# A two-step state space recurrence, and an fp32r scatter of the experts' results in two passes

## What is computed

```
def s5_mixer(u, lam_re, lam_im, b, c, d_skip, log_dt, w_glu, b_glu):   # 64 groups of 16 channels, 64 states each
    dt = exp(log_dt); a = exp((lam_re + 1j * lam_im) * dt)             # one complex factor per state
    b_bar = (a - 1) / lam * b
    x[t] = a * x[t - 1] + b_bar @ u[t]                                 # for 256 tokens t
    y[t] = real(c @ x[t]) + d_skip * u[t]
    g = gelu(y)
    val, gate = split(g @ w_glu + b_glu)
    return val * sigmoid(gate)

def moe_ffn(u, w_router, w13, w2):                                     # top 2 of 8 experts
    top_val, top_idx = top_k(u @ w_router, 2); top_w = softmax(top_val)
    out = 0
    for e in range(8):
        gate_e = sum(where(top_idx == e, top_w, 0))
        out += gate_e[:, None] * swiglu(u, w13[e], w2[e])
```

## Time and profile before

| | |
|---|---|
| median of 3 runs | 2593.39 us (2592.49 to 2596.54) |
| the profiled execution, its own time | 2592.58 us |
| its span in the trace | 2590.5 us, 31848 instructions |
| PE busy | 2421.6 us (93%) |
| DVE busy | 1809.1 us (70%) |
| ACT busy | 1261.3 us (49%) |
| POOL busy | 159.4 us (6%) |
| mean granted clock of PE | 0.961 of full speed |
| read from HBM | 583.60 MB, 226 GB/s over the span |

### The profile page before, as it was taken

How to read it: one execution, slowest core, us unless ns; L and a number is a source line. 1 busy time by engine, 2 the same in 40 slices (tenths; PEclk the granted TensorE clock), 3 DMA queues, 4 the chain that set the end, 5 groups by cost and what they waited for, 6 DMA issues and landing times.

```text
span 2590.5 us, 31848 instructions
## 1 busy us (share of the span) xinstructions
PE 2421.6 (93%) x12441; PEld 1937.3 (75%) x12441; DVE 1809.1 (70%) x1966; ACT 1261.3 (49%) x1290; POOL 159.4 (6%) x142
## 2 busy tenths in 40 slices
PE   7999999999999999989989965689999999999996
PEld 6878858788878678789658852367888887887885
DVE  5763348857852477685545459968888888898887
ACT  3432334334322434344334444537667677776674
POOL 0000000000000000000100006500000000000000
PEclk9999999999999999999999985789999999999998
DMA  9767158657756287543245530138999989998994
GB/s 315 257 230 181 50 180 287 248 205 274 258 162 150 66 280 272 195 170 115 98 155 188 178 121 33 65 122 281 336 338 345 347 319 348 350 343 323 344 345 176
DMA packets 303413, 586.14 MB, mean 226 GB/s; under 512 B 61439, under 2 KB 96965, under 8 KB 303181
## 3 DMA queue, kind: packets, MB, share of 16 engines
q1 hardware_dynamic: 285954, 521.09, 58.0%
q0 software_dynamic: 16928, 63.46, 7.4%
q10 hardware_dynamic: 428, 0.15, 0.0%
HBM read 583.60 MB, written 1.06 MB: 226 GB/s over the span
## 4 chain that ended last, share of the span: by engine, by line
PE 84%; DVE 10%; ACT 3%; issue 2%; DMA 1%; DVEq 0%; SPq 0%; ACTq 0%
PE psum L862 19%; PE psum L864 19%; PE psum L863 19%; PE psum L1326 3%; PE psum L895 3%; PE psum L1333 2%; PE psum L1388 2%; PE psum L2049 2%; PE psum L985 2%; DVE ring_r L1062 2%; PE psum L2673 2%; PE psum L2828 1%; PE psum L2851 1%; ACT ring_r L1056 1%; PE psum L1946 1%
## 5 line engine op out<-in xcount | busy, mean ns | idle before, releaser
L1062 DVE TENSOR_TENSOR ring_r<-ring,ring_r 128x2048 fp32r<-128x2048 f32 x286 | 652.6, 2289 | 291.4 <-ACT ring_r L1056 291.0
L1056 ACT CAST ring_r<-ring 128x2048 fp32r<-128x2048 f32 x286 | 545.2, 1910 | 507.3 <-PE psum L864 412.8
L864 PE MATMUL psum<-ring_r,arena_r 128*128 128x512 f32 (+1 forms) x1560 | 596.9, 383 | 0.0
L862 PE MATMUL psum<-ring_r,arena_r 128*128 128x512 f32 (+1 forms) x1016 | 400.3, 394 | 10.1 <-DVE arena_r L2846 5.2
L1062 DVE TENSOR_TENSOR ring_r<-ring,tail_r 128x2048 fp32r<-128x2048 f32 x143 | 327.2, 2288 | 95.9 <-ACT tail_r L1056 95.8
L863 PE MATMUL psum<-ring_r,arena_r 128*128 128x512 f32 (+1 forms) x1016 | 390.6, 384 | 0.0
L1056 ACT CAST tail_r<-ring 128x2048 fp32r<-128x2048 f32 x143 | 273.2, 1910 | 145.3 <-PE psum L864 139.3
L864 PEld LDWEIGHTS psum<-ring_r,arena_r 128*128 128x128 f32 x1560 | 294.4, 189 | 58.4
L864 PE MATMUL psum<-ring_r,z_r 128*128 128x512 f32 (+1 forms) x840 | 310.6, 370 | 0.0
L862 PEld LDWEIGHTS psum<-ring_r,arena_r 128*128 128x128 f32 x1016 | 192.3, 189 | 57.9 <-issue 18.5
L863 PEld LDWEIGHTS psum<-ring_r,arena_r 128*128 128x128 f32 x1016 | 192.3, 189 | 37.7 <-issue 1.9
(11 more groups left out here) (436 smaller groups left out, 3293.9 us busy)
## 6 DMA issues: line engine op xcount, KB each, us to landing
ring<-in_moe_w SPq DMA_DIRECT2D x264, 1024.0 KB, 6.9
arena<-in_ada_w POOLq DMA_DIRECT2D x48, 1024.0 KB, 9.2
ring<-in_ffn_wg SPq DMA_DIRECT2D x44, 1024.0 KB, 7.4
ring<-in_ffn_wu SPq DMA_DIRECT2D x44, 1024.0 KB, 7.3
ring<-in_ffn_wd SPq DMA_DIRECT2D x44, 1024.0 KB, 7.0
ring<-in_ffn_w SPq DMA_DIRECT2D x33, 1024.0 KB, 5.6
ring<-in_mlstm_w_in SPq DMA_DIRECT2D x8, 2048.0 KB, 8.6
ring<-in_mlstm_w_out SPq DMA_DIRECT2D x4, 2048.0 KB, 9.1
```

Source lines behind the costliest of these rows:

```text
L862: pe.matmul(dst, lhs_low, rhs, start=start, stop=False)
L864: return pe.matmul(dst, lhs, rhs_low, start=False, stop=stop)
L1056: act.copy(upper[i % UPPERS], place(PN[r.key, i])).then_inc(upper_ready, 1)
L1062: dve.tensor_tensor(low, raw, upper[i % UPPERS], ALU.subtract).then_inc(lower_ready, 1)
```

## The change

Two things are changed.

**The recurrence takes two tokens per step.** With PAIRS = 128, a state at an even token 2m follows from that at 2m - 2 with the squared factor, driven by `a b_bar u[2m - 1] + b_bar u[2m]`. So `inputs` now adds two products per state (with `BT` of two kinds, `b_bar` and `a b_bar`), and everything between it and `outputs` has 128 columns in place of 256: the phases, the rotations, DVE's four operations, the scans (now with `l_mag2`, the squared magnitude) and POOL's two products. The odd tokens are computed from the even ones: `y[2m + 1] = real(c a x[2m]) + real(c b_bar) u[2m + 1]`. POOL makes `c a` as `CT_next` (five operations per k, `c{k}`), PE makes the kernel `real(c b_bar)` (`same_step`, eight small matmuls, into `bank(7)`, which DVE clears once), ACT copies it (`copy_kernel`), and `outputs` has three parts: the even tokens (16 matmuls of 128 columns), one full matmul with the kernel, and the odd tokens (16 more, which wait for `c{k}`). `scanned` has eight places instead of four. `s5_scale_b_dve` is called with a piece 0 to 3, in `ffn_dve` of `ffn4` behind the half-panels 26 to 29, instead of all at once after `ffn4`, and makes twice as much (`b_wide` and `b_next`). The second half of the turned B (`bt4` to `bt7`) is made inside the recurrence. C's load waits for the end of `ffn4` instead of `bt3`. ACT's gelu of the first half stands earlier in its stream, the gated product uses other PSUM banks, and its second high half no longer waits for the last unit.

**The scatter is fp32r in two passes.** `scatter` is now a 0/1 matrix in fp32r; `y_part` is the high part of an expert's result and `y_low` the rest, which DVE subtracts (`lower_y_dve`, two operations per expert on a new semaphore `half_lowered`). `scatter_pe` issues four fp32r matmuls per half instead of two fp32 ones, and the gate is applied by DVE when it adds (`scattered_dve`). `route_dve` clears more.

The diff, cut to its core:

```diff
+            if r.n == 4 and "s5" in stages and UP_HALVES + 4 <= i < UP_HALVES + 8:
+                s5_scale_b_dve(dve, step, i - UP_HALVES - 4)
...
+        for out_, other, op in ((l_kr2, l_ki, ALU.subtract), (l_ki2, l_kr, ALU.add)):
+            dve.tensor_tensor(l_t1, l_lr, l_kr if out_ is l_kr2 else l_ki, ALU.mult)
+            link(dve.tensor_tensor(l_t2, l_sin, other, ALU.mult))
+            link(dve.tensor_tensor(out_, l_t1, l_t2, op))
...
+            if k >= 2 and n % 2 == 0:
                 pool.wait_ge(*s5P.after(f"y{k - 2}"))
-            pool.tensor_tensor(prods[k % 2][:, 0:2, j, :], scanned[:, n % 4, :, :, :], both(r[:, 0, :, :]), ALU.mult)
-            pool.tensor_tensor(prods[k % 2][:, 2:4, j, :], scanned[:, n % 4, :, :, :], both(r[:, 1, :, :]), ALU.mult)\
-                .then_inc(*s5G.inc(f"x{n}"))
+            pool.tensor_tensor(prods[:, k % 2, 0:2, j, :], scanned[:, n % 8], both(r[:, 0]), ALU.mult)
+            pool.tensor_tensor(prods[:, k % 2, 2:4, j, :], scanned[:, n % 8], both(r[:, 1]), ALU.mult).then_inc(*s5G.inc(f"x{n}"))
+            if n % 2 == 0:
+                continue
+            c, after = CT[:, k % 2], CT_next[:, k % 2]
+            pool.wait_ge(*s5A.after(f"ct{k}"))
+            if k >= 1:
+                pool.wait_ge(*s5G.after(f"c{k - 1}"))
+            pool.tensor_tensor(after, c, lam_of(l_lr, k, 3), ALU.mult)
+            pool.tensor_tensor(c_part, c[:, 0:2], lam_of(l_sin, k, 2), ALU.mult).then_inc(*step.one())
+            pool.wait_ge(*step.now())
+            pool.tensor_tensor(after[:, 0], after[:, 0], c_part[:, 1], ALU.add)
+            pool.tensor_tensor(after[:, 1], after[:, 1], c_part[:, 0], ALU.subtract)
+            pool.tensor_tensor(after[:, 2], after[:, 2], c_part[:, 1], ALU.subtract).then_inc(*s5G.inc(f"c{k}"))
...
-                act.activation(phase[:, j, :], const("steps"), ACT.Identity, scale=turns)
-                ins = act.activation(whole[:, j, :], const("steps"), ACT.Identity, scale=turns, bias=eps[:, 4:5])
+                act.activation(phase[:, j, :], steps, ACT.Identity, scale=turns)
+                ins = act.activation(whole[:, j, :], steps, ACT.Identity, scale=turns, bias=eps[:, 4:5])
...
+        def copy_kernel(k):
+
+            act.wait_ge(*s5P.after(f"kb{k}"))
+            act.copy(kernel_0[:, k % 2, :], bank(7)[:, SEQ:SEQ + P]).then_inc(*s5A.inc(f"kc{k}"))
...
             place_c(k)
+            if k >= 1:
+                copy_kernel(k - 1)
             if k + 1 < KD:
                 rotations(k + 1)
+            else:
+                gelu(act, 0)
+            if k == 0:
+                copy_b(6)
+                copy_b(7)
+        copy_kernel(KD - 1)
...
-            dve.scalar_tensor_tensor(xT[:, k, :], xT[:, k, :], col_a("s5_d", k), bank(6)[:, 0:SEQ], ALU.mult, ALU.add)\
+            steps_of = xT[:, k, :].rearrange("p (m i) -> p m i", i=2)
+            dve.scalar_tensor_tensor(steps_of, steps_of, col_a("s5_d", k),
+                                     bank(6 - k % 2)[:, 0:SEQ].rearrange("p (i m) -> p m i", i=2),
+                                     ALU.mult, ALU.add)\
...
-            dve.tensor_tensor(by_cos, bu, both(r[:, 0, :, :]), ALU.mult)
-            dve.tensor_tensor(bu, bu, both(r[:, 1, :, :]), ALU.mult).then_inc(*s5V.inc(f"w{n}"))
+            dve.tensor_tensor(cosines, bu, both(r[:, 0]), ALU.mult)
+            dve.tensor_tensor(bu, bu, both(r[:, 1]), ALU.mult).then_inc(*s5V.inc(f"w{n}"))
...
-                mag = l_mag[:, state:state + 1].to_broadcast([P, SEQ])
+                mag = l_mag2[:, state:state + 1].to_broadcast([P, PAIRS])
                 for i in range(2):
-                    ins = dve.tensor_tensor_scan(scanned[:, n % 4, i, jj, :], mag, bu[:, 1 - i, jj, :], 0.0, ALU.mult, ALU.add)
+                    ins = dve.tensor_tensor_scan(scanned[:, n % 8, i, jj, :], mag, bu[:, 1 - i, jj, :], 0.0, ALU.mult, ALU.add)
             ins.then_inc(*s5V.inc(f"scan{n}"))
-            if n % 2 and k >= 1:
-                skip_u(k - 1)
+            if n % 2 and k >= 2:
+                skip_u(k - 2)
...
         low_x(0)
+        skip_u(KD - 2)
         glu_lower_dve(dve, 0)
         skip_u(KD - 1)
...
-            pe.wait_ge(*s5A.after(f"ct{k}"))
             pe.wait_ge(*s5G.after(f"x{2 * k + 1}"))
-            if k >= 1:
-                pe.wait_ge(*s5V.after(f"y{k - 1}"))
+            if k < 2:
+                pe.wait_ge(*s5A.after("bt7"))
+            else:
+                pe.wait_ge(*s5V.after(f"y{k - 2}"))
+            even, odd = (bank(6 - k % 2)[:, i * PAIRS:(i + 1) * PAIRS] for i in range(2))
             for i, v in enumerate((0, 1, 1, 2)):
                 for j in range(QUAD):
-                    own_rows = slice(32 * j, 32 * j + 32)
-                    mm = pe.matmul(bank(6)[own_rows, 0:SEQ], CT[:, k % 2, v, j, :], prods[k % 2][:, i, j, :],
-                                   start=i == 0, stop=i == 3)
+                    pe.matmul(even[channels(j), :], CT[:, k % 2, v, j, :], prods[:, k % 2, i, j, :], start=i == 0, stop=i == 3)
+            pe.wait_ge(*s5A.after(f"kc{k}"))
+            pe.matmul(odd, kernel_0[:, k % 2, :], x_at[:, k, 1, :], start=True, stop=True)
+            pe.wait_ge(*s5G.after(f"c{k}"))
+            for i, v in enumerate((0, 1, 1, 2)):
+                for j in range(QUAD):
+                    mm = pe.matmul(odd[channels(j), :], CT_next[:, k % 2, v, j, :], prods[:, k % 2, i, j, :],
+                                   start=False, stop=True, skip_group_check=True)
             mm.then_inc(*s5P.inc(f"y{k}"))
...
+            pe.wait_ge(*s5A.after(f"ct{k}"))
+            if k >= 1:
+                pe.wait_ge(*s5A.after(f"kc{k - 1}"))
+            for part in range(2):
+                for j in range(QUAD):
+                    mm = pe.matmul(bank(7)[channels(j), SEQ + 32 * j:SEQ + 32 * j + 32],
+                                   b_wide[:, part, QUAD * k + j, :, :].rearrange("p g h -> p (g h)"), CT[:, k % 2, part, j, :],
...
+            for i in range(2):
+                for j in range(2):
+                    rows_ = channels(2 * u + j)
+                    pe.matmul(driven(n)[:, i, j, :], BT[rows_, 0, i, k, :], x_at[rows_, k, 0, :], start=True, stop=True)
+                for j in range(2):
+                    rows_ = channels(2 * u + j)
+                    mm = pe.matmul(driven(n)[:, i, j, 1:PAIRS], BT[rows_, 1, i, k, :], x_at[rows_, k, 1, 0:PAIRS - 1],
+                                   start=False, stop=True, skip_group_check=True)
...
+        for n in range(S5_UNITS + 1):
+            k, odd = divmod(n, 2)
             if n < S5_UNITS:
                 inputs(n)
-                if n % 2:
-                    turn_c(n // 2)
-            if n % 2 == 0 and n >= 4 and n // 2 - 2 < KD - 1:
-                outputs(n // 2 - 2)
+            if n in (0, 2):
+                for i in (4 + n, 5 + n):
+                    if n == 2:
+                        pe.wait_ge(*s5A.after(f"bt{i - 2}"))
+                    turn_b(pe, i)
+            if (odd or n == S5_UNITS) and k >= 1:
+                same_step(k - 1)
+            if odd:
+                turn_c(k)
+            elif k >= 2:
+                outputs(k - 2)
...
-        dve.memset(scatter, 0.0)
-        dve.memset(y_part, 0.0).then_inc(half_copied, 2)
-        dve.memset(y_sum[:, :, :], 0.0)
+        dve.memset(late_gate[:, :, 0:1], 0.0)
+        link(dve.memset(y_sum[:, :, :], 0.0))
+        dve.tensor_copy(scatter, y_sum[:, 0, 0:NT * P])
+        dve.tensor_copy(y_low, y_sum[:, 1, :])
+        dve.tensor_copy(y_part, y_sum[:, 1, :]).then_inc(half_lowered, 2)
...
-        pe.wait_ge(half_copied, 2 * e + (half + 1))
-        for t in range(NT):
-            mm = pe.matmul(bank((6, 4)[half] + t), scatter[:, t * P:(t + 1) * P], y_part[:, half * 512:(half + 1) * 512],
-                           start=True, stop=True)
+        pe.wait_ge(half_lowered, 2 * e + (half + 1))
+        for t in range(NT):
+            for part in (y_part, y_low):
+                mm = pe.matmul(bank((6, 4)[half] + t), scatter[:, t * P:(t + 1) * P], part[:, half * 512:(half + 1) * 512],
+                               start=part is y_part, stop=part is y_low)
...
             part = y_sum[:, t, half * 512:(half + 1) * 512]
-            ins = dve.tensor_tensor(part, part, bank((6, 4)[half] + t), ALU.add)
+            gate = late_gate[:, t, e:e + 1] if isinstance(e, int) else late_gate[:, t, bass.ds(e, 1)]
+            ins = dve.scalar_tensor_tensor(part, bank((6, 4)[half] + t), gate, part, ALU.mult, ALU.add)
...
+        for half in range(2):
+            lower_y_dve(dve, e, half)
```

230 lines of the change are left out of this document (138 added, 92 removed).

## The result

| | before | after |
|---|---|---|
| median of the runs | 2593.02 us (2592.49 to 2596.54, 4 runs) | 2536.54 us (2535.22 to 2537.18, 4 runs) |
| the profiled execution, its own time | 2592.58 us | 2537.16 us |
| its span | 2590.5 us | 2535.4 us |
| mean granted clock of PE | 0.961 | 0.971 |

The ratio is 0.9777, with a 95% interval from 0.9762 to 0.9792. The forecast was 2530 us with a range of 2518 to 2552: right in direction and range, 6.5 us too low. The two profiled executions are 55.4 us apart, where the sum said 63.0.

A forecast was written before the change was run, and what follows sets the result against it. It took DVE to bound the recurrence and PE the experts. From 2592.6 us, -49.8 (recurrence) - 2.7 + 1.1 + 0.9 - 12.9 - 1.0 + 1.4 = -63.0, rounded 2530 us; range 2518 to 2552.

The forecast's parts named there:

- POOL becomes the bound: Recurrence: POOL's work of 8.15 us per k sets the pace, with DVE close behind at 7.9.
- The first phases, -2.4 and -2.7: Ahead of POOL's stretch: first phases and rotations half as wide, -2.4 us; DVE's first unit 3.4 for 6.1, -2.7.
- The tail, -2.4: Behind POOL's end: only the odd part of the last `outputs` follows, 1.5 us in place of 3.93, so -2.4.
- The sum by the rule of the Trainium skill: Recurrence's end: by the exclusive port lock the last `c a` waits out a whole `low_x`; total 2531.8 us.
- Discretization, +1.1: `mlstm`: six more DVE operations of 0.19 us precede a low part PE already waits for; +1.1 us, unhidden.
- B's scaling, -2.7: End of `ffn4`: pieces before the last four low parts fill DVE's idle time; -2.7 us, or as little as 0.
- router, +0.9: Router: more is cleared where PE and DVE are level; +0.9 us, from 0.3 to 1.3.
- The scatter, -12.9 - 1.0 + 1.4: Experts: 1.62 us less per expert, -12.9 for eight; -1.0 behind the last; 1.4 given back for weight transfers.
- Rival C: Experts gain nothing, as DVE or the weights' transfer take PE's place; +14 us, 2544; chance 0.12.
- A (the low clock stays): Recurrence: PE stays at the low clock, a k takes 10.9 us; 2552 us; chance 0.14.
- B (a k of 9.3): Recurrence loop: DVE and POOL delay each other; 2539 us; chance within the 0.66 shared with the forecast.
- D (17): Recurrence: the engines' work of one k stops overlapping, a k takes 17.0 us; 2601 us, slower; chance 0.03.

The follow-up runs named there:

- pool_double: The changed kernel with POOL's product of 128x384 made twice in each k, with a wait between the two; 2540.72 us.
- angle_early: The changed kernel with DVE's `angle(k + 1)` behind the scans of the step's first unit, not between the operations of its second; 2533.94 us.
- before_six: The kernel before with six more DVE operations of 128x32 at the same place in `mlstm`, results unused; 2598.01 us, ratio 1.0019.
- scatter_only: The kernel before with the change to the experts alone (fp32r scatter in two passes, gate at the addition, router's clears); 2585.56 us, ratio 0.9969.
- no_c7: The changed kernel without four of POOL's five `c a` operations for the last k; 2538.49 us.
- bias_late: The changed kernel with ACT's two copies for the bias row moved behind the first two high parts of the gated product's weights; 2533.87 us.
- s5_only: The changed kernel with the experts as before (plain fp32 scatter), without the router's new clears; 2547.32 us, ratio 0.9821.
- add_late: The changed kernel with DVE adding the scattered halves behind half-panels 6 and 8 of the next expert, not 2 and 4; 2542.09 us.
- moves_and_split: The changed kernel with `angle`, bias copies and six discretization operations moved, scattered halves added behind half-panels 2 and 8; 2528.44 us, ratio 0.9749.

## Why the prediction was right, and where it was off

**Direction and size: right.** A k came to 8.08 us against the 8.15 of the sum. POOL's stretch came to 68.2 against 68.5, and that is luck: eight k of POOL's work are 61.5 and not 65.2, its waits for DVE 3.5 and not 3.3, and its last operations are held off for 3.0 more, which the sum had at nothing. DVE's terms held one by one: a 512 wide pair 0.61 and 0.72, a 256 wide one 0.34 and 0.46, four scans 1.27 against 1.3, a unit 3.4.

**"POOL becomes the bound": wrong, hidden in a right number.** The step that failed is first the price of `c a`, 3.05 us. A line through POOL's two forms of product (1.26 at 512, 2.35 at 1024) gave 0.99 and 0.72 for 384 and 256 elements; they take 0.79 and 0.70 from start to start, the three narrow ones 0.41 each and not 0.45, so `c a` is 2.7 and POOL's k 7.7 us. The 0.4 between that and the 8.08 is DVE's wait for ACT, which was in the rows of before (0.61 at the end of a k) and which I had used as an allowance and not as a ring. pool_double and angle_early show both.

**The first phases, -2.4 and -2.7: a term too large by 1.1.** Of the 5.1 itself 0.3 did not come. The rest stands ahead of it: ACT takes 2.9 us for its four copies of turned B, where it took 2.2, and waits 0.27 for PE twice in between. That is not the change's work. PE turns B with the same 16 matmuls, in 3.38 us in place of 2.54, as its low clock reaches to 1541.8 us, through nearly all of them, and before only to 1539.7; before_six and scatter_only, with the old recurrence, have copies of 2.8 and 3.2 us in the same way.

**The tail, -2.4: the term that failed most in the recurrence, -0.6.** The 1.5 us held only if PE is free when POOL ends. PE had 6.2 us of the gated product to do ahead of the last `outputs`, begun 4.11 us late by ACT's order (no_c7, bias_late). POOL is held off for 3.0 us there beside DVE, 1.0 on its last product and 2.0 on `c a`, where the sum had no delay; but no_c7 shows that this alone costs nothing. The sum by the rule of the Trainium skill ("SBUF — State Buffer", section "SBUF: two separate sides") had such a delay, and POOL's 3.0 us agree with it in kind.

**Discretization, +1.1: right as work, 1.1 us, and short of its clock.** PE's wait, at 2.5 us, is followed by the low level, 1.5 us more at the spot; before_six shows it on the kernel before. Another 1.6 us are lost 200 us later, behind a wait of 2.54 us that is there before and after, with a fall of the clock in eight of fourteen kernels. Why it fell in these and not in the others is open.

**B's scaling, -2.7, measured -2.6; router, +0.9, measured 0:** s5_only, without the clears, takes the same time there.

**The scatter, -12.9 - 1.0 + 1.4: measured -8.1 - 1.0.** Of the 1.62 per expert 0.2 is missing at the halves themselves, most of it behind the first, and 0.40 is DVE's queue, as add_late and moves_and_split show by moving the late matmuls with its additions. Rival C had the mechanism (DVE takes PE's place), its size is a quarter of the gain and not all of it.

**The rivals.** A (the low clock stays): the clock alternated, 0.76 in the mean of the stage, not the 0.9 I named. But PE had 5.0 to 5.5 us of work at the high level and was never what a k waited for. B (a k of 9.3) and D (17) did not come; `outputs` found `c a` ready in the loop, but for 0.41 us of waiting at the last k but one.

## What to carry to other kernels

When two engines have nearly the same work per step, double an operation on one of them: if the step grows by less than the operation, that engine had room, and where the other waits too, a wait between engines may be the bound. Then moving the instruction that feeds that wait one place up may be worth more than making either engine faster. A microsecond of DVE work ahead of a low part that PE already waits for can cost several (5.1 us for 1.1 here), as PE's clock may fall behind a wait of 2.5 us, and may not. Work that is moved onto an engine with idle time pays back part of the gain wherever that engine runs without a gap for some 20 us: ask where the next idle time is, not how much there is in all.

## What the runs showed of the hardware that I had not expected

PE's clock behind a wait in full work: early in `mlstm` it fell in seven of seven executions after 2.50 to 2.61 us, and in none of seven after 2.06 us or less; at 1344 us, behind one and the same wait of 2.54 us, it fell in eight of fourteen. So the length of a wait alone does not tell whether the clock falls. The Trainium skill ("TensorE: Matmul & The Clock Gate", Part 1) says that activity releases a throttle that is the default; these runs agree in kind. One of POOL's operations of 128x128 took 2.50 us in place of 0.46 beside a DVE operation with both inputs in SBUF. And executions of the same code lie up to 1.5 us apart already before `mlstm`: differences below 2 us between single executions say little here, and the profile's own distances from instruction to instruction say more.
